# Normalizing the second row tile of the residual stream: from ScalarE to VectorE, in a two-layer hybrid encoder on one core

## The reference

```python
def _layer_norm(x, g, b):
    mu = jnp.mean(xf, -1, keepdims=True)
    var = jnp.mean(jnp.square(xf - mu), -1, keepdims=True)
    return (xf - mu) * lax.rsqrt(var + LN_EPS) * g + b

def reference(...):
    for l in range(DEPTH):                      # DEPTH = 2
        m = mod[:, 0]
        y = _swiglu(_modulate(x, m), ffn_w_up[l, 0], ffn_w_down[l, 0])
        x = _layer_norm(ALPHA * x + 0.5 * (1.0 + m[:, 2]) * y, ln_g[l, 0], ln_b[l, 0])
        m = mod[:, 1]
        y = _mixer(_modulate(x, m), w_in[l], ...)   # attention, stick-breaking, gated DeltaNet
        x = _layer_norm(ALPHA * x + (1.0 + m[:, 2]) * y, ln_g[l, 1], ln_b[l, 1])
        m = mod[:, 2]
        y = _swiglu(_modulate(x, m), ffn_w_up[l, 1], ffn_w_down[l, 1])
        x = _layer_norm(ALPHA * x + 0.5 * (1.0 + m[:, 2]) * y, ln_g[l, 2], ln_b[l, 2])
```

## Time and profile before

| what | value |
|---|---|
| median of three runs | 1442.05 us |
| time of the profiled execution | 1442.05 us |
| its span, first to last instruction | 1440.2 us |
| PE busy | 1343.5 us, 93% |
| DVE busy | 987.1 us, 69% |
| ACT busy | 673.8 us, 47% |
| POOL busy | 120.3 us, 8% |
| mean granted TensorE clock | 0.978 of full speed |

### The profile page before, as it was taken

How to read it: one execution, slowest core, us unless ns; L and a number is a source line. 1 busy time by engine, 2 the same in 40 slices (tenths; PEclk the granted TensorE clock), 3 DMA queues, 4 the chain that set the end, 5 groups by cost and what they waited for, 6 DMA issues and landing times.

```text
span 1440.2 us, 17703 instructions
## 1 busy us (share of the span) xinstructions
PE 1343.5 (93%) x6916; PEld 1130.9 (79%) x6916; DVE 987.1 (69%) x1230; ACT 673.8 (47%) x985; POOL 120.3 (8%) x216
## 2 busy tenths in 40 slices
PE   2899999899899899999999999989989988999997
PEld 2688887898699677888878888879868976788885
DVE  6577755777666676788467876459767657676555
ACT  0644434668433445444354444356664343544441
POOL 4001001000000010001100000100000000010000
PEclk9999999999899999999999999999989999999999
DMA  9688872866454438888559887376653443496550
GB/s 352 217 280 266 279 246 74 282 214 192 132 160 148 145 95 262 277 282 281 178 164 303 267 282 270 91 253 204 216 177 119 144 147 117 162 308 201 176 196 38
DMA packets 194082, 295.18 MB, mean 205 GB/s; under 512 B 14248, under 2 KB 158160, under 8 KB 194000
## 3 DMA queue, kind: packets, MB, share of 16 engines
q1 hardware_dynamic: 173488, 220.57, 45.9%
q0 software_dynamic: 20512, 73.48, 17.0%
HBM read 292.97 MB, written 1.05 MB: 204 GB/s over the span
## 4 chain that ended last, share of the span: by engine, by line
PE 82%; ACT 6%; DVE 5%; issue 3%; DMA 2%; SPq 2%; POOL 0%; POOLq 0%; ACTq 0%; DVEq 0%
PE pg L904 68%; PE pt L1222 1%; PE pt L1210 1%; ACT lnw L491 1%; PE pt L929 1%; PE pt L864 1%; DMA wraw<-in_w_in_dram 1%; PE pt L1220 1%; SPq L253 1%; ACT whi L509 1%; DMA wraw<-in_ffn_w_up_dram 1%; DVE wlo L1453 1%; PE pt L873 1%; PE pt L1069 1%; SPq L261 1%
## 5 line engine op out<-in xcount | busy, mean ns | idle before, releaser
L1453 DVE TENSOR_TENSOR wlo<-wraw,whi 128x1024 fp32r<-128x1024 f32 (+1 forms) x408 | 480.0, 1200 | 210.6 <-ACT whi L509 210.3
L509 ACT ACTIVATE whi<-wraw 128x1024 fp32r<-128x1024 f32 (+1 forms) x408 | 405.9, 1035 | 229.2 <-PE pg L904 135.1
L904 PE MATMUL pg<-whi,hhi 128*128 128x512 f32 x1056 | 425.5, 403 | 15.8 <-DVE hlo L1441 9.3
L904 PE MATMUL pg<-wlo,hhi 128*128 128x512 f32 x1056 | 414.6, 393 | 0.0
L904 PE MATMUL pg<-whi,hlo 128*128 128x512 f32 x1056 | 414.6, 393 | 0.0
L904 PEld LDWEIGHTS pg<-whi,hhi 128*128 128x128 f32 x1056 | 200.8, 190 | 59.2 <-DVE hlo L1441 11.6
L904 PEld LDWEIGHTS pg<-whi,hlo 128*128 128x128 f32 x1056 | 200.1, 190 | 43.1
L904 PEld LDWEIGHTS pg<-wlo,hhi 128*128 128x128 f32 x1056 | 201.0, 190 | 39.2 <-issue 0.5
L1477 DVE SCALAR_TENSOR_TENSOR acc<-aw,sc,acc 128x1024 f32<-128x1024 f32 x128 | 163.5, 1278 | 0.0
L904 PE MATMUL pg<-whi,athi 128*128 128x512 f32 x352 | 140.7, 400 | 0.0
L904 PE MATMUL pg<-wlo,athi 128*128 128x512 f32 x352 | 139.1, 395 | 0.0
(11 more groups left out here) (309 smaller groups left out, 1350.5 us busy)
## 6 DMA issues: line engine op xcount, KB each, us to landing
wraw<-in_ffn_w_up_dram SPq DMA_DIRECT2D x176, 512.0 KB, 5.6
aw<-in_w_ada_dram POOLq DMA_DIRECT2D x128, 512.0 KB, 4.5
wraw<-in_w_in_dram SPq DMA_DIRECT2D x104, 512.0 KB, 5.0
wraw<-in_ffn_w_down_dram SPq DMA_DIRECT2D x88, 512.0 KB, 4.7
pro<-in_w_ada_dram SPq DMA_DIRECT2D x8, 1024.0 KB, 14.4
wraw<-in_w_branch_dram SPq DMA_DIRECT2D x16, 512.0 KB, 4.4
wraw<-in_w_o_dram SPq DMA_DIRECT2D x16, 512.0 KB, 4.0
lnw<-in_ln_g_dram POOLq DMA_DIRECT2D x5, 512.0 KB, 4.1
```

What stands on the lines that cost most here:

```text
L509: act.activation(hi_view(n)[:, 0:size], wraw[:, q, o:o + size], ACT.Copy).then_inc(S["w_hi"], 1)
L904: ins = pe.matmul(out_ap, a[i], b[j], start=first and n == 0, stop=last and n == 2, skip_group_check=group)
L1453: dve.tensor_tensor(lo, a, hi_view(n)[:, 0:size].bitcast(F32), ALU.subtract).then_inc(S["w_lo"], 1)
```

## The change

For t = 1, at the five passages between stages, x is normalized by VectorE with the routine that t = 0 uses already. The two activations of ScalarE, the small one that makes `nmr`, VectorE's `negmu`, and the two tiles and two semaphores that belonged to them are gone. The last stage did this already and stays as it is.

```diff
@@ ScalarE, norm_stage
                     split(2 * u_next + 3)
                     modulate(at, s, 0, 0)
                     modulate(at, s, 0, 1)
-                    act.wait_ge(S["ln_rstd"], at("ln_rstd", NT * s + 2))
-                    act.wait_ge(S["ln_neg"], at("ln_neg", s + 1))
-                    act.activation(nmr[:, :], negmu[:, :], ACT.Copy, scale=rstd[:, 1:2]).then_inc(S["ln_nmr"], 1)
-                    act.wait_ge(S["ln_nmr"], at("ln_nmr", s + 1))
-                    for n in (0, 1):
-                        c = slice(n * 512, (n + 1) * 512)
-                        act.activation(x[:, 1, c], x[:, 1, c], ACT.Identity, bias=nmr[:, 0:1],
-                                       scale=rstd[:, 1:2]).then_inc(S["ln_x"], 1)
                     modulate(at, s, 1, 0)
                     modulate(at, s, 1, 1)
@@ VectorE, norm_stage
                     h_low(at, s, 0, 1)
                     residual(1, 1)
                     moments(1)
-                    dve.wait_ge(S["ln_mv"], at("ln_mv", NT * s + 2))
-                    dve.tensor_scalar(negmu[:, :], mv[:, 1, 0:1], -1.0, None, ALU.mult).then_inc(S["ln_neg"], 1)
+                    normed(1)
                     h_low(at, s, 1, 0)
                     h_low(at, s, 1, 1)
```

More of the change, by code:

```diff
@@ L30 @@
 PER = {
-    "prm_in": 64, "ln_rows": 96, "ln_rstd": 6, "ln_var": 6, "ln_neg": 3, "ln_nmr": 3,
+    "prm_in": 64, "ln_rows": 96, "ln_rstd": 6, "ln_var": 6,
     "x_gain": 6, "o_rs": 2, "h_f32": 12, "h_hi": 12, "w_hi": 204, "up_silu": 44, "act_hi": 22, "mix_ev": 14, "sm_T": 1, "sm_in": 1,
@@ L157, in trunk @@
         rstd = sb("rstd", [P, NT])
-        negmu = sb("negmu", [P, 1])
-        nmr = sb("nmr", [P, 1])
         mhalf = sb("mhalf", [P, 8])
```

## The result

The changed kernel is slower: 1452.62 us as the median of four runs (1451.91 to 1454.49), beside 1442.99 us for the kernel before in the same comparison; ratio 1.0065, 95% interval 1.0044 to 1.0087. That is 9.6 us more, where 2.85 us less was forecast, and it lies outside the range. The profiled execution took 1451.06 us with a span of 1449.3 us, 9.1 us more than before. One run of the kernel before, of 1961.34 us at a mean granted clock of 0.654, belongs to a second, slow state and is left out of every median and ratio in this document.

What follows compares the result with a forecast made beforehand. TensorE, busy 93% of the span, was taken as the bound, waiting for ScalarE's activation at five passages. Five gains of 0.57 us make 2.85 us: 1442.05 - 2.85 = 1439.2 us, range 1437.0 to 1442.1 us.

Steps and rivals of the forecast that it cites:

- Nothing else is on the path: Claim, after five passages at 0.57 us gave 2.85 us, that no other work changes the kernel's time.
- what is removed: At each passage, rstd's start to the first transpose's weight load: 1.78 us through nmr and ScalarE's first activation on x.
- The new chain: At each passage, rstd's start to the transposes' weight load with VectorE normalizing x: between 1.19 and 1.26 us.
- The gain of a passage: Time saved at each of five passages between stages: between 0.52 and 0.59 us, taken as 0.57 us.
- The instruction: VectorE's normalization of one 512-column half of x at t = 1: 0.54 us, as measured at t = 0.
- the cover: VectorE's idle time before t = 1's first low part absorbs the added 1.00 us; some 2.5 us left.
- The clock: TensorE half-clock stretches, 3.2 us each, appear or vanish: one fewer 9%, one more 6%, two more 5% (1445.6 us, slower).
- my signs of being wrong: Transpose later than 1.3 us after rstd, modulation later than 0.76 us behind it, or half-clock sums differing beyond the gain.
- The rival of a second strand: An equally long strand behind ScalarE's keeps TensorE waiting at the passages: no effect, 1442.05 us, 5%.
- that of transfers: Mixer weight loads after the first and fourth passage take back two gains: 1.7 us left, 1440.3 us, 11%.
- The rule on two-port modes: VectorE's tensor_scalar in a two-port mode locks out GpSimd; no cost expected, since no GpSimd work lies beside it.
- the estimate of 0.27 us: Rival: VectorE's 512-column instruction takes half of 0.54 us, gaining 0.27 us more a passage; 1437.9 us, 4%.

Runs made afterwards that it cites:

- the three versions with both tiles kept: Changed kernel plus two unused one-column tiles where negmu and nmr stood; alone, all tiles 64 bytes higher, all 384 higher: ratios 0.9963, 0.9956, 0.9960 to the kernel before.

## Why the prediction was wrong, point by point

**The step that failed** is the sentence in the sum, "Nothing else is on the path", together with the item in what is removed: two one-column tiles were priced by their instructions alone. Their bytes were priced at nothing. Taking them away moved `whi2`, `athi` and `atlo` by 64 bytes against `whi`, `wlo`, `hhi` and `hlo`, and the 512-column matmuls of the FFNs and of the mixers' input products got slower: by 3.0 ns a step in the mean in the groups of h, most of it where `whi2` is read (6.9 ns), and by 3.7 ns in those of the gated product. By the gaps this is 1056 x (1.5 + 3.8 + 3.7) = 9.5 us in the groups of h and 352 x (3.9 + 3.9 + 3.4) = 3.9 us in those of the gated product, 13.4 us. Less 2.95 us at the passages that is +10.5 us; measured were +9.6 us. The addresses alone, without the moved work, cost 0.80% = 11.5 us in their own run.

**What held.** The new chain was put between 1.19 and 1.26 us, taken as 1.21, and was 1.18 to 1.20 us. The gain of a passage was 0.59 us, the upper bound given, where 0.57 was taken. The instruction took 544 ns, neither faster nor slower at the new place, as the 14 instances of t = 0 had said. VectorE's idle time before the low part fell from 4.75 to 2.55 us (forecast: about 2.6), so the cover held. TensorE's idle time before the transposes fell to 0.67 us, for a forecast of 0.77. From the transposes to the first modulation it was 0.76 us in all five passages, as forecast. One thing forecast to stay didn't: the idle time before the first matmul on t = 1 grew from 0.94 us to 1.18 us. The eight transposes took 1.11 us instead of 1.36 us, since their second half of x is ready in time now; TensorE runs through them and through the fourth weight half sooner and waits longer for the low part. The idle times alone would have given 0.67 - 0.24 = 0.43 us a passage; the chain gave 0.59 us, and that is what the anchors show.

**The rivals.** The clock was the rival on the slower side, with 5 in 100. A half-clock stretch did appear before the first passage, at full clock in the kernel before:

```profile
217.00:221.00 4.00, 4.00 (x13) 3.09 (x12) 3.57 (x4) 0.13 (x1) 3.48 (x3) 0.59 0.00 0
```

```profile
217.00:221.00 4.00, 4.00 (x19) 3.32 (x18) 2.81 (x3) 1.69 (x2) 1.48 (x3) 1.00 0.01 3
```

The first row is of after, the second of before. It is part of the 3.84 us at the first passage: the unchanged kernel's second profile has such a stretch too and starts this rstd at 242.52 us, 1.27 us later than its first. One of my signs of being wrong was a sum of half-clock stretches that differs by more than the gain, and it does, 93.6 us after against 65.7 us before. But 27.3 us of that is one stretch from 20 us on, in which TensorE works 13.03 of 28 us (12.61 before), and the unchanged kernel's second profile has the same stretch, 93.1 us in all, and took 1440.73 us. So the clock isn't the cause of the 9.6 us: the loss stands in windows whose clock is 1.00 in both kernels, and it goes when 64 bytes are put back and nothing else is changed. The rival of a second strand is refuted by the five passages. Against that of transfers, which would have left 1.7 us (0.12%), stand the three versions with both tiles kept, whose intervals all end at or below 0.9979; since part of their gain is unexplained, this is no proof. That the change could harm work it doesn't touch, through the place of the data, was not among my cases, and the evidence that it might was in the diff: two declarations gone, in the middle of a list.

**VectorE's rate.** The rule on two-port modes led me to ask only what VectorE's instruction does to GpSimd. The five passages neither confirm nor refute the lock, as no GpSimd work lay beside it. The prediction set the measured 0.54 us against the estimate of 0.27 us and found twice as much. That comparison was wrong, as an instruction's duration also holds a part that doesn't grow with its columns. Another tensor_scalar of the same trace shows it, at two widths (busy us, mean ns, idle time before):

```profile
L1678 DVE TENSOR_SCALAR scr<-scr,frec 128x256 f32<-128x256 f32 x8 | 2.3, 350 | 0.1
L1678 DVE TENSOR_SCALAR scr<-scr,frec 128x128 f32<-128x128 f32 x8 | 1.7, 288 | 0.1
```

128 more columns cost 62 ns, 0.48 ns each. And the second half of x starts 0.46 us after the first (1.00 us for both, less 0.54 us), 0.90 ns a column. The Trainium skill, "VectorE: DVE Perf Modes", section "Mode 2×_2P — use both read ports for one tensor", has two results per cycle for such an instruction; at the page's clock of 0.96 GHz one result per cycle would be an estimated 1.04 ns a column. Both rows are faster than that, so they agree with the page and not with one element at a time. The forecast's 0.54 us was a measured duration and isn't touched by this.

## What to carry to other kernels

Removing or adding a small tile moves everything declared behind it. Before a change is judged, keep the places of the big operands (a tile of the same size where the old one was), and after it compare how many equal instructions an always busy engine gets done in equal windows at equal clock. A local gain that shows in every passage and a time that goes the other way mean that the loss is in work which the diff doesn't name.

## What the runs showed of the hardware

- Matmuls that stream 512 fp32r columns past a 128x128 stationary tile mostly started 226 or 227 ns apart (means 226.5 to 227.7 ns) when the byte addresses of all operands' tiles differed by multiples of 256, and more slowly in every other arrangement tried (stationary less moving 64, 128, 192 and 224 modulo 256). With every pair at 64 it was 233.3 ns in the mean, 2.6% slower; with every pair at 128, 232.4 ns; with every pair at 192, 229.7 ns. Absolute places of 0, 128 and 192 modulo 256 (all tiles together) made no difference. What in the memory or in TensorE's reading causes it isn't shown, nor why one distance costs more than another, nor how unequal distances in a sequence combine.
- The slow step isn't confined to the instruction with the odd distance: with a third of the pairs off, all three kinds of matmul in the sequence slowed from 227.5 to 228.5 - 229.7 ns.
- Twelve runs of one kernel against 22 of its twin gave a ratio of 0.9983. Single runs of the kernel before ranged over 12 us, from 1437.75 to 1449.88 us.
- A float32 tensor_scalar of VectorE took 288 ns for 128 columns and 350 ns for 256, and two of 512 columns started 0.46 us apart while each lasted 0.54 us.
